# A transformer kernel with its RMS roots taken late: token-wise sums on TensorE, first panels ahead of the norm sum

## The reference, cut to what matters

```
y = x * rsqrt(mean(x*x) + 1e-6) * g            # rms_norm
ffn   x + 0.5*rms(swiglu(rms(x)))              # D_FF 2816
mixa  x + rms(rwkv7 || conv of rms(x) @ w_in)
mixc  x + rms(forgetting attention of rms(x) @ w_in)
mixb  x + hybrid_mixer(rms_2(x))               # no norm behind it
mem   x + cross_attention(rms_2(x), mem)
ffnc  x + conv_gated_ffn(rms_2(x))
order: ffn mixa ffn ffn mixc ffn mixb mem ffnc mixb mem ffnc, then a final rms_norm_2
```

## Time and profile before

| | |
|---|---|
| median of 3 runs | 4197.38 us (4197.2 to 4206.96) |
| span of the profiled execution | 4201.7 us |
| PE busy | 3849.5 us, 92% of the span |
| DVE, ACT, POOL busy | 2091.9, 1506.0 and 50.1 us |
| chain that ended last | PE 86%, DVE 9%, ACT 3% |
| idle of PE ahead of L323, most of it behind POOL | 100.5 us |

### The profile page before, as it was taken

How to read it: one execution, slowest core, us unless ns; L and a number is a source line. 1 busy time by engine, 2 the same in 40 slices (tenths; PEclk the granted TensorE clock), 3 DMA queues, 4 the chain that set the end, 5 groups by cost and what they waited for, 6 DMA issues and landing times.

```text
span 4201.7 us, 52276 instructions
## 1 busy us (share of the span) xinstructions
PE 3849.5 (92%) x19654; PEld 3114.4 (74%) x19654; DVE 2091.9 (50%) x3029; ACT 1506.0 (36%) x2228; POOL 50.1 (1%) x56
## 2 busy tenths in 40 slices
PE   8998949978998999898998998898999997899998
PEld 6886838856886888697566886766788885687886
DVE  4434384555434443423535434445677435457763
ACT  3323330133323332334333333354544235545432
POOL 0000000000000000000000000000000000000000
PEclk9998965579999999898989998999999998999999
DMA  3332300002332333221012332201233330032332
GB/s 121 99 96 70 95 17 1 1 26 75 96 95 79 94 96 93 78 90 55 1 36 75 95 95 82 64 1 51 81 97 98 94 97 21 1 101 80 100 92 88
DMA packets 83794, 296.83 MB, mean 71 GB/s; under 512 B 9472, under 2 KB 9472, under 8 KB 83136
## 3 DMA queue, kind: packets, MB, share of 16 engines
q1 hardware_dynamic: 82080, 288.24, 22.5%
q0 software_dynamic: 1568, 6.56, 0.5%
HBM read 292.66 MB, written 2.10 MB: 70 GB/s over the span
## 4 chain that ended last, share of the span: by engine, by line
PE 86%; DVE 9%; ACT 3%; issue 1%; DMA 0%; POOL 0%; SPq 0%; DVEq 0%; ACTq 0%
PE PS L244 20%; PE PS L245 20%; PE PS L253 20%; PE PS L753 3%; PE PS L776 3%; PE PS L285 3%; PE PS L286 2%; PE PS L288 2%; PE PS L765 1%; PE PS L755 1%; PE PS L843 1%; PE PS L323 1%; DVE WK L470 1%; PE PS L1646 1%; PE PS L1657 1%
## 5 line engine op out<-in xcount | busy, mean ns | idle before, releaser
L244 PE MATMUL PS<-WK_R,WHI 128*128 128x512 f32 (+1 forms) x3832 | 1492.3, 390 | 45.4 <-ACT WK_R L513 35.0
L245 PE MATMUL PS<-WK_R,WLO 128*128 128x512 f32 (+1 forms) x3832 | 1486.8, 389 | 0.0
L220 DVE TENSOR_TENSOR WLO<-RAW,WHI 128x1024 fp32r<-128x1024 f32 x563 | 689.6, 1225 | 1309.7 <-ACT WHI L216 1307.1
L216 ACT ACTIVATE WHI<-RAW 128x1024 fp32r<-128x1024 f32 x563 | 595.7, 1058 | 1113.5 <-PE PS L253 888.0
L244 PEld LDWEIGHTS PS<-WK_R,WHI 128*128 128x128 f32 x3832 | 721.8, 188 | 207.9 <-issue 49.3
L245 PEld LDWEIGHTS PS<-WK_R,WLO 128*128 128x128 f32 x3832 | 722.0, 188 | 146.9 <-issue 1.7
L253 PE MATMUL PS<-H_LO,WHI 128*128 128x512 f32 x2712 | 672.9, 390 | 1.0 <-DVE H_LO L375 0.6
L253 PEld LDWEIGHTS PS<-H_LO,WHI 128*128 128x128 f32 x2712 | 509.4, 188 | 109.4 <-DVE H_LO L375 2.9
L253 PE MATMUL PS<-HID_LO,WHI 128*128 128x512 f32 x1056 | 262.8, 389 | 0.0
L285 PE MATMUL PS<-WHI,WK_R 128*128 128x256 f32 (+1 forms) x832 | 223.6, 299 | 20.5 <-ACT WK_R L351 17.1
L253 PEld LDWEIGHTS PS<-HID_LO,WHI 128*128 128x128 f32 x1056 | 198.3, 188 | 41.0
(11 more groups left out here) (282 smaller groups left out, 3708.5 us busy)
## 6 DMA issues: line engine op xcount, KB each, us to landing
RAW<-in_ffn_gu SPq DMA_DIRECT2D x176, 512.0 KB, 3.6
RAW<-in_f_up SPq DMA_DIRECT2D x88, 512.0 KB, 3.5
RAW<-in_ffn_dn SPq DMA_DIRECT2D x64, 512.0 KB, 3.5
RAW<-in_c_in SPq DMA_DIRECT2D x32, 512.0 KB, 3.6
RAW<-in_f_dn SPq DMA_DIRECT2D x32, 512.0 KB, 3.5
RAW<-in_ffn_dn SPq DMA_DIRECT2D x32, 384.0 KB, 3.1
RAW<-in_a_in SPq DMA_DIRECT2D x22, 512.0 KB, 3.6
RAW<-in_b_out SPq DMA_DIRECT2D x16, 512.0 KB, 3.7
```

The source lines that it names most:

```text
L216: nc.scalar.activation(WHI[:, slot, :], RAW[:, slot, :], ACT.Copy).then_inc(S("w_hi"), 1)
L220: nc.vector.tensor_tensor(WLO[:, slot, :], RAW[:, slot, :], WHI[:, slot, :].bitcast(F32), ALU.subtract).then_inc(S("w_lo"), 1)
L244: pe.matmul(o, WHI[:, slot, w], hi(k), start=(first and b_ == 0), stop=False)
L245: pe.matmul(o, WLO[:, slot, w], hi(k), start=False, stop=False)
```

## The change

`LATE_ROOT` is gone: every phase feeds its products with x times gain, and scales what comes out. mixa does so with a DVE multiply per panel, mixc and mixb with four ACT copies per panel in place of one. In mixa the sigmoid of four tiles moves behind the last panel.

The sums are turned: the block of squares is the weight and a column of ones moves, so that the sum of each token stands on a partition, in a 128x4 tile (`token_sums`, four matmuls of one column). Root and reciprocal act on 128x4, and four matmuls with the identity spread the reciprocal over the partitions again (`token_spread`). GpSimd adds nothing any more; each tile has its own sum.

The first panel runs tile by tile behind the new x, with the sum of each tile between its products (`first_tiles`, `first_tokens`). In the chain behind an output the squares come straight from PSUM, the sum of the first seven tiles is taken inside the last product, and the gain goes into ACT's copy. At the start of the program ACT splits the first two weight pieces ahead of the eight squares. The output is stored in four transfers of 512 KB in place of one of 2 MB.

The diff's core (indented less than in the file; removed lines are mostly left out):

```
+def first_tiles(pe, p, n, tiles):
+    pe_bank(pe, p)
+    pe.wait_ge(S("w_lo"), p.N + tiles)
+    for k in range(DT):
+        w = slice(128 * k, 128 * k + 128)
+        pe.wait_ge(S("norm_hi"), DT * n + k + 1)
+        for i in range(tiles):
+            slot, o = p.nslot(i), bank(p.slot, i)
+            pe.matmul(o, WHI[:, slot, w], h_hi(k), start=(k == 0), stop=False)
+            pe.matmul(o, WLO[:, slot, w], h_hi(k), start=False, stop=False)
+        norm_add(pe, p, n, k)
+    for i in range(tiles):
+        feature_lo(pe, p, i, h_lo, range(DT), True, i, fresh=h_fresh(n))
+        if i == 0:
+            norm_spread(pe, p, n)
+def first_tokens(pe, p, n, pieces, cols):
+    def part(s_, last_part):
+        slot = p.nslot(s_)
+        if not last_part:
+            pe.wait_ge(S("w_lo"), p.N + (s_ + 1))
+        for b_, k in enumerate(pieces[s_]):
+            w = slice(cols * b_, cols * b_ + cols)
+            pe.wait_ge(S("norm_lo" if last_part else "norm_hi"), DT * n + k + 1)
+            for t in range(TT):
+                o = PS[:, 4 * p.slot + t, 0:cols]
+                if last_part:
+                    mm = pe.matmul(o, h_lo_t(k, t), WHI[:, slot, w], start=False, stop=(k == DT - 1))
+                else:
+                    pe.matmul(o, h_hi_t(k, t), WHI[:, slot, w], start=(k == 0), stop=False)
+                    pe.matmul(o, h_hi_t(k, t), WLO[:, slot, w], start=False, stop=False)
+            if not last_part and s_ < 2:
+                norm_add(pe, p, n, k)
+    part(0, False)
+    part(1, False)
+    part(0, True)
+    for k in sum((list(ks) for ks in pieces[2:]), []):
+        norm_add(pe, p, n, k)
+    if len(pieces) == 2:
+        norm_spread(pe, p, n)
+    part(1, True)
+    if len(pieces) == 3:
+        norm_spread(pe, p, n)
+        part(2, False)
+        part(2, True)
+    pe.wait_ge(S("norm_rs"), n + 1)
...
 def norm_square(act, pos, k):
     wait_x(act, pos, k)
-    nc.scalar.activation(SC[:, k, :], X[:, k, :], ACT.Square).then_inc(S("norm_squares"), 1)
-    if late(pos):
+    if pos < len(plan):
         gain = input_gain(*plan[pos][:2])
         nc.scalar.activation(WK_R[:, XHI + k, :], X[:, k, :], ACT.Copy, scale=gain(k)).then_inc(S("norm_hi"), 1)
-def norm_pairs(pool, n):
...
-def norm_add(pe, P0, k, first):
-    mm = pe.matmul(bank(P0 % 2, 3), ones, SC[:, k, :], start=first, stop=(k == DT - 1))
+    nc.scalar.activation(SC[:, k, :], X[:, k, :], ACT.Square).then_inc(S("norm_squares"), 1)
+def token_sums(pe, b_, k, first, last):
+    for t in range(TT):
+        mm = pe.matmul(PS[:, b_, t:t + 1], SC[:, k, 128 * t:128 * t + 128], ones[:, 0:1], start=(first and t == 0),
+                       stop=(last and t == TT - 1))
+    return mm
+def token_spread(pe, b_, r):
+    for t in range(TT):
+        mm = pe.matmul(PS[:, b_, 128 * t:128 * t + 128], r[:, t:t + 1].to_broadcast([128, 128]), ident, start=True, stop=True)
+    return mm
+def norm_add(pe, p, n, k):
+    pos = n
+    if early(pos):
+        if k < DT - 2:
+            return
+        if k == DT - 2:
+            pe.wait_ge(S("norm_running"), (DT - 2) * (early_before[pos] + 1))
+            token_sums(pe, spare(p, 3), 0, True, False)
+            return
+    pe.wait_ge(S("norm_squares"), DT * n + k + 1)
+    mm = token_sums(pe, spare(p, 3), k, k == 0, k == DT - 1)
     if k == DT - 1:
         mm.then_inc(S("norm_sum"), 1)
+def norm_spread(pe, p, n):
+    pe.wait_ge(S("norm_recip"), n + 1)
+    token_spread(pe, spare(p, 2), NRM[:, 1, :]).then_inc(S("norm_spread"), 1)
...
+    if pos == 0:
+        split_hi(act, 0, 0, 0)
+        split_hi(act, 1, 0, 1)
     if not early(pos):
         for k in range(DT):
             norm_square(act, pos, k)
-    if pos == 0:
-        split_hi(act, 0, 0, 0)
-        split_hi(act, 1, 0, 1)
     act.wait_ge(S("norm_sum"), n + 1)
+    nc.scalar.activation(NRM[:, 0, :], PS[:, 4 * (1 - P0 % 2) + 3, 0:TT], ACT.Sqrt, bias=eps[:, 0:1], scale=1.0 / D).then_inc(S("norm_root"), 1)
+def norm_copy(act, n, P0):
+    act.wait_ge(S("norm_spread"), n + 1)
+    nc.scalar.activation(RS[:, 1, :], PS[:, 4 * (1 - P0 % 2) + 2, :], ACT.Copy).then_inc(S("norm_rs"), 1)
...
+def norm_recip(dve, n):
+    dve.wait_ge(S("norm_root"), n + 1)
+    nc.vector.reciprocal(NRM[:, 1, :], NRM[:, 0, :]).then_inc(S("norm_recip"), 1)
+def norm_dve(dve, n, gain):
     for k in range(DT):
         dve.wait_ge(S("norm_hi"), DT * n + k + 1)
         nc.vector.scalar_tensor_tensor(out=H_LO[:, k, :], in0=X[:, k, :], scalar=gain(k), in1=WK_R[:, XHI + k, :].bitcast(F32),
                                        op0=ALU.mult, op1=ALU.subtract).then_inc(S("norm_lo"), 1)
+        if k == 4:
+            norm_recip(dve, n)
...
+        feature_hi(pe, p, s_, hi, k, s_ == 0, fresh=f)
+        if between and s_ == len(ks) - 1:
+            between()
+        feature_lo(pe, p, s_, lo, k, s_ == len(ks) - 1, fresh=f)
...
+    def early_sums():
+        pe.wait_ge(S("post_running"), (DT - 2) * (m + 1))
+        token_sums(pe, sums, 0, True, False)
+        out_product(pe, kind, out_panel(where, d), hi, lo, fresh, early_sums if d == DT - 1 else None)
     pe.wait_ge(S("post_squares"), DT * (m + 1))
-    pe.matmul(PS[:, 3, :], ones, SC[:, DT - 1, :], start=False, stop=True).then_inc(S("post_sum"), 1)
+    token_sums(pe, sums, DT - 1, False, True).then_inc(S("post_sum"), 1)
+    pe.wait_ge(S("post_recip"), m + 1)
+    token_spread(pe, 4 * last.slot + 2, PST[:, 1, :]).then_inc(S("post_spread"), 1)
...
+        nc.scalar.activation(SC[:, d, :], bank(p.slot), ACT.Square).then_inc(S("post_squares"), 1)
+        if d < DT - 1:
+            nc.scalar.activation(F[:, d, :], bank(p.slot), ACT.Copy, scale=gain(d)).then_inc(S("panel_out"), 1)
+        ahead(split_hi, act, p, n - 1)
     act.wait_ge(S("post_sum"), m + 1)
-    nc.scalar.activation(RS[:, 0, :], PS[:, 3, :], ACT.Sqrt, bias=eps[:, 0:1], scale=1.0 / D).then_inc(S("post_root"), 1)
+    nc.scalar.activation(PST[:, 0, :], PS[:, 4 * p.slot + 1, 0:TT], ACT.Sqrt, bias=eps[:, 0:1], scale=1.0 / D).then_inc(S("post_root"), 1)
+    nc.scalar.activation(F[:, DT - 1, :], bank(p.slot), ACT.Copy, scale=gain(DT - 1)).then_inc(S("panel_out"), 1)
...
+        if d < DT - 1:
+            ahead(split_lo, dve, p, last)
     dve.wait_ge(S("post_root"), m + 1)
-    nc.vector.reciprocal(RS[:, 1, :], RS[:, 0, :]).then_inc(S("post_recip"), 1)
-    dve.wait_ge(S("post_recip"), m + 1)
-    for k in range(DT):
-        nc.vector.scalar_tensor_tensor(out=F[:, k, :], in0=F[:, k, :], scalar=gain(k), in1=RS[:, 1, :],
-                                       op0=ALU.mult, op1=ALU.mult).then_inc(S("post_scaled"), 1)
+    nc.vector.reciprocal(PST[:, 1, :], PST[:, 0, :]).then_inc(S("post_recip"), 1)
+    ahead(split_lo, dve, p, last)
+    dve.wait_ge(S("post_spread"), m + 1)
+    def add(k):
         dve.wait_ge(S("post_scaled"), DT * m + k + 1)
         nc.vector.tensor_tensor(X[:, k, :], X[:, k, :], F[:, k, :], ALU.add).then_inc(S("x_post"), 1)
+    for k in range(DT):
+        dve.wait_ge(S("panel_out"), p.P0 - (DT - 1) + k + 1)
+        nc.vector.tensor_tensor(F[:, k, :], F[:, k, :], PS[:, 4 * p.slot + 2, :], ALU.mult).then_inc(S("post_scaled"), 1)
+        if k > 0:
+            add(k - 1)
+    add(DT - 1)
...
+        if p.is_first():
+            norm_copy(act, b["norm"], b["P"])
...
+        for i in range(DT // 2):
+            sp.wait_ge(S("out_made"), 2 * i + 2)
+            sp.dma_start(out[:, 2 * i:2 * i + 2, :], H[:, 2 * i:2 * i + 2, :]).then_inc(S("stored"), 16)
+        sp.wait_ge(S("stored"), 16 * (DT // 2))
...
+        norm_recip(dve, NN)
+        dve.wait_ge(S("norm_spread"), NN + 1)
+        for k in range(DT):
+            nc.vector.scalar_tensor_tensor(out=H[:, k, :], in0=X[:, k, :], scalar=vec("fin", k), in1=PS[:, 4 * (1 - NP_ % 2) + 2, :],
+                                           op0=ALU.mult, op1=ALU.mult).then_inc(S("out_made"), 1)
...
+        for t in range(TT):
+            d = dst[:, t, bass.ds((p.e - 4 * i) * 256, 256)]
+            o = nc.scalar.activation(d, PS[:, 4 * p.slot + t, 0:256], fn, scale=env["NRM"][:, 1, t:t + 1])
+        o.then_inc(S("panel_out"), 1)
...
+act.wait_ge(S("panel_out"), P + 22)
+for f in range(4):
+    sc.activation(cgate[:, f, :], cgate[:, f, :], ACT.Sigmoid).then_inc(S("cgate_made"), 1)
...
+def plain(p):
+    env["ahead"](env["split_lo"], dve, p, 0)
+    dve.wait_ge(S("piece_done"), p.N + 1)
+    tt(at_tile(HID, 0, p.e), bank(p.slot), RS[:, 1, :], ALU.mult).then_inc(S("panel_out"), 1)
```

More of the change, by code:

```diff
@@ L273, in token_piece @@
-        def token_piece(pe, p, s_, hi, lo, ks, cols, first, last, tiles=TT, fresh=None):
+            for i in range(2):
+                feature_piece(pe, p, i, h_hi, h_lo, range(DT), True, True, i)
+        def first_tiles(pe, p, n, tiles):
[13 more added lines that the diff above has]
+                    norm_spread(pe, p, n)
@@ L275, in token_piece @@
+        def token_piece(pe, p, s_, hi, lo, ks, cols, first, last, tiles=TT):
             slot = p.nslot(s_)
```

(27 more changed lines are left out.)

218 lines of the change are left out of this document (88 added, 130 removed).

## The result

The changed kernel takes 4275.02 us in the median of 4 runs (4244.94 to 4305.04); the kernel before, run beside it, 4202.17 (4197.2 to 4272.63). The ratio is 1.0171, 95% interval 1.012 to 1.0222. It is slower, as forecast. The forecast of 4243 met the lower level; the upper one it did not know. The median lies inside the stated range (4175 to 4278) by 3 us and outside the narrower one of the forecast (4222 to 4272), and its place there is luck: it is the middle of two executions at either level, and the next four executions of the same kernel have their median at 4316. The profiled execution is one of the upper level, 4302.71 us, span 4300.9.

What follows compares the result with a forecast made beforehand. PE products fill the time (86% of the chain), so gains lie where PE stands still between phases. Terms sum to +45.3 on the span of 4201.7, 4247; less 4.3 for span over median, 4243 us; range 4175 to 4278.

Steps and rivals of the forecast that it cites:

- start: Program start: PE waits for both WLO, second panel at 52.4 where it was 30.54; +22 us.
- post to mixa: Boundary into mixa: next panel at E+33.7, was 40.2; following panel's slow start gives back 2; -4.5 us.
- post to ffn, three: Three boundaries into ffn: slow mixed panel, next panel at E+43.0 where it was E+36.2; +6.8 each, +20.5 us.
- post to mixc, mixb: Boundaries into mixc and mixb: next panel E+42.8, was 45.1, and E+47, was 47.9; -1.5 and -1 us.
- mem to ffnc, two: Two residual boundaries: wait for both WLO, two sums, late H_LO, spread, clock; +8 each, +16 us.
- mixb to mem, two: Two residual boundaries where H_LO steps set the pace and the spread is added; +2 us.
- ffnc to mixb: Residual boundary: no reciprocal of 3.3, no normalized tile ahead of PE, but sums and a spread; -6 us.
- inside mixa (its tail): Mixa's tail: a scale and four sigmoids of 0.6 ahead of tanh; +3 us.
- The rival on the other side, the clock that comes back: At the first tiles of seven panels, the clock returns inside the mixed panel: -34, 4163 us; chance 0.16.
- The rival of cheap sums: 56 sums in the mixed panels cost 0.85 at either clock: 34 us less, 4209; chance 0.08.
- E+8.5: Post boundaries: PE starts the panel 8.5 us after E, the last output product's end (before the change); was E+24.6.
- the row 2116 to 2146: Mixc's attention: PE fully busy with small fp32 matmuls, clock 0.50 throughout; evidence that the mixed panel stays at 0.50.

Runs made afterwards that it cites:

- the run on the start: Changed kernel with ACT's old order at program start and the first norm's eight sums ahead of the WLO wait: 4233.03, 4234.74 us, others 4289; ratio 1.0138.
- the half waits: Changed kernel, first panel behind mixb, mem and ffnc run by tile halves, each with its own WLO wait: 4234.81 and 4240.53 us in the lower level, ratio 1.0081.
- The filled wait: One unread 256-column matmul ahead of one wait per head in mixc's attention: 4226.8 us on the changed kernel, 4187.99 us on the kernel before.
- the held clock alone: Kernel before with nine unread 512-column matmuls behind the last output sum at the six post boundaries: 4202.01 us, ratio 1.0006.
- the chain with the gap filled: Changed kernel with unread constant matmuls in the three waits behind an output: 4174.79 us, ratio 0.992, one execution at 4229.03.
- the wide sums: Changed kernel with 128 columns of ones instead of one in each tile's sum between the first products: 4173.25 us, ratio 0.9914 to before.

## Why the prediction was right, and where it was not

The terms against the two profiles, in microseconds. Both kernels run the same 4536 matmuls of the low passes (H_LO or HID_LO with WHI) in the same order, so the lag of the changed kernel can be read at each; a term is what the lag gains from the last output panel ahead of a boundary to the second panel behind it.

| term | forecast | measured |
|---|---|---|
| start | +22 | +22.3 |
| post to mixa | -4.5 | -7.2 |
| post to ffn, three | +20.5 | +5.9, +4.8, +6.5 = +17.2 |
| post to mixc, mixb | -1.5, -1 | -1.7, -3.3 |
| mem to ffnc, two | +16 | +7.1, +5.7 = +12.8 |
| mixb to mem, two | +2 | +5.0 |
| ffnc to mixb | -6 | -7.4 |
| final norm | -6 | -5.2 |
| inside mixa (its tail) | +3 | +6.7 |
| mixc ahead of its attention | +0.8 | 0.0 |
| elsewhere | 0 | +0.9 |
| sum of these | +45.3 | +40.1 |
| attention of mixc | 0 | +59.1 here, -0.7 in the lower level |

The last row is of this profile, of the upper level; the -0.7 is from the traces of the run on the start and of the half waits, both of the lower one. 40.1 and 59.1 are the 99.2 by which the two spans differ. Of mixa's 6.7, 3.6 are the longer wait ahead of the first matmuls behind tanh, and 2.2 the first five of these, since the clock fell in that wait (before, then with the change):

```profile
535.70 2.38 PE L1585 MATMUL PS<-HID,WK 64*128 64x512 f32 x5 [2.19 <-ACT HID L1704]
...
554.42 4.60 PE L1687 MATMUL PS<-HID,WK 64*128 64x512 f32 x5 [5.79 <-issue]
```

In the lower level the change thus costs some 40 us against the profiled execution of before, but 4245 stands 48 above 4197. The profiled execution was not one of those at 4197: in the executions of this kernel beside the experiments the time is 2.4 us above the span, so its span of 4201.7 stands for some 4204, 7 above. 40 and 7 place the 48 to within the 2 us by which the traces differ among themselves. That 4243 comes so near the lower level is luck in part: my sum was 5 too large, and I took 4.3 off the span where the time of the changed kernel is 1.8 above it.

**Right:** at the ffn boundaries the first panel begins 16 to 17 us sooner and the next one later; the clock is 0.50 from the start to the end of the products and sums in turn at all seven places (by the record at six, by the prices at the start); the start; mem to ffnc with its five idle microseconds, which the second and third of the windows above show with the clock behind them. The rival on the other side, the clock that comes back, didn't happen in the changed kernel. It is no empty rival: held up across the gap, the clock stays up in the same panel (4160 to 4177).

**Sizes:** a one-column record costs 0.213 at the low clock and 0.114 at the high one, 1.70 and 0.91 a group; I had 1.45 and 0.85. The straight line through the rows of the attention was too low below and, for 128 columns, too high above (0.174 against 0.11). The rival of cheap sums is out: 0.85 at either clock isn't so. The Trainium skill ("TensorE: Matmul & The Clock Gate", on LDWEIGHTS) gives a weight load as its columns over 1.2 GHz, with no other figure for the low clock; the 107 ns that I estimate from it for 128 columns are near the record of 0.114 at 1.00 and far from that of 0.213 at 0.50. The other errors go the other way: the first product came at E+7.9 and not at E+8.5 (the parts that I listed come to E+8.2), the spread cost 1.4 at that boundary and not 2.3, and the second low pass ran at the full clock already.

**What failed:** the step from the sum to "4243", in which the attention of mixc stands at nothing. It is right for three of the eight executions of the changed kernel. I used the row 2116 to 2146 for the panel, and not for the place where it stood: an attention in which the clock, once fallen, can stay at 0.50 for long. That it could do so for 181 us, and that the change could move the moment at which it falls, was open to be asked; it cost 57 to 60 us in three of the eight executions, 86 in two, and 70 to 76 in 7 of 50 of the kernel before. Theory M, that a clock which fell there doesn't come back, goes too far: the low stretches in this attention last 14, 31, 48, 58, 65, 164 and 181 us in the traces. What ends them, and why the long ones come more often after the change, isn't settled. The filled wait shows which waits let the clock fall (in the profiles of both kernels the longest stretch begins within 1.5 us of the end of one of them), not why a given execution hits them.

By the same page of the Trainium skill ("What's actually happening") activity releases the clock. These traces don't bear that out as it stands: TensorE is busy for 25.00 of 25.00 us in the panel and for 180.00 of 180.00 in the attention, and the clock stays at 0.50 in both. With 128 columns in the small matmuls the same panel came up at its second tile.

The longest low stretch of all was touched by no run: inside mixa the clock is at 0.50 for 263 to 266 us on end in every profile, before and after, and TensorE is busy for about nine tenths of it. A window of the kernel before that holds most of it:

```profile
580.00:860.00 280.00, 244.93 (x2608) 214.15 (x2608) 161.11 (x267) 29.76 (x59) 0.00 (x0) 0.52 0.01 1
```

## What to carry to other kernels

When work is moved into a place where TensorE waits, ask which clock it will run at there and what stands between the large products: here groups of one-column matmuls went with 1.2 GHz for 25 us at a time, and 128 columns in their place cost nothing more at the full clock and won 72 us. A short chain and a held clock belong together: here the chain alone cost 39 to 48 us and the held clock alone won nothing, while the chain with the gap filled was 0.8% faster than before, and 2% with the start, the half waits, the wide sums and the filled attention. Where executions fall on levels, look for a stretch in which the engine is busy and the granted clock stays at 0.50, and fill the wait ahead of it.

## What the hardware showed that I had not expected

- The same products and sums run a whole panel at either clock: tiles of 3.41 us at 0.50 and of 1.83 at 1.00, by what stood ahead of them (at five boundaries of six).
- A record of a full-precision matmul with new 128x128 weights (two to a matmul) takes 0.11 us at the full clock for 1 column and for 128; with 1 column it takes 0.21 at the low one.
- One idle wait of 0.84 us in an attention of small matmuls was followed, 1.4 us behind its end, by 181 us at half the clock, and a filler of 256 columns per head made six executions agree within 1.1 us.
